# Boundary between the two layers cut from 14 steps to 11, row work through full PSUM pairs, and the last residual sum made by an accumulating DMA

## The chip, the cores and the metric

The kernel runs on one core of one Trainium2 chip. The metric is the device time of one execution in microseconds (us), lower is better. The profile of one execution shows TensorE (PE, with its weight loads as PEld), VectorE (DVE), ScalarE (ACT), GpSimd (POOL) and the DMA queue of SyncE (SP).

## The reference, cut to what matters

A batch of one sequence, 1024 rows by 1024 features in float32, passes two layers. Each layer is `x = x + rms_norm(mixer(rms_norm(x, pre_g)), post_g)`.

```python
for l in range(2):
    h = rms_norm(x, pre_norm_g[l])
    if l == 0:   # heads A (differential, 4) and B (sliding window, 8) beside each other
        y = concat([ya * silu(ga), yb * silu(gb)]) @ w_out_ab
    else:        # C: chunked attention over 9 chunks, 16 heads, relative-position bias
        y = (yc * silu(gc)) @ w_out_c
    x = x + rms_norm(y, post_norm_g[l])
```

Each of q, k, v and the gates is a projection `h @ w_in` of the normalised rows. So nothing of layer 2 can be projected for a row before layer 1 is complete for that row: its output sum, two norms and a transpose.

## The kernel before, in words

All products run on TensorE with each float32 operand cut into a high and a low part, three matmuls for one product (hi*hi, hi*lo, lo*hi). The cut of the weights is made by GpSimd (`split`, L906 the high part, four instructions on L913 the low part), the cut of everything that comes out of PSUM by ScalarE (high) and VectorE (low).

The work is laid out by hand in numbered steps. Every engine walks through the same steps in order and issues in each what the tables name for it; semaphores carry the true dependences. The units are A[0..3] (20 steps each), B[0..7] (8 steps each, steps 80 to 143), then a boundary of `BRIDGE` = 14 steps (144 to 157), then C[0..7] (20 steps each, C[0] from step 158). An attention item of a unit starts in each of its first 16 steps (8 for B): `score` (L1192), the lowest value on VectorE (L1555), the exponential on ScalarE (L1287), `turn` (the transposition of the probabilities, L1162), their cut (L1316 on ScalarE, L1619 on VectorE), `times_v` (L1118), a gate (`gated` on VectorE L1669, `hi_of_gated` on ScalarE, `gated_lo` on VectorE), and the output projection `out_matmuls` (L1045).

Between items TensorE works on fills. A fill is 24 matmuls of 128x512 (L1037, `project`) that make one half (f=0: rows 0 to 3 of 128, f=1: rows 4 to 7) of q, k, v or gate of one unit. `segment` and `segment_by` say how many of these matmuls each step gets. Fills go in turn to two PSUM banks (`dense` 0 and 1). Their weights lie in two high slots (`w_hi`) used in turn: the split of one block may start only when the last fill that used the same slot is finished. `split` stands in GpSimd's queue at a step of its own, behind the roots of the norms of that step.

The third bank (`dense` 2) serves the output projections, one half row at a time, and in the same way the transposes that bring the second layer's normalised rows back (`spare_use`). Each use waits until the one before has been read. If a step has two uses, one goes ahead of the step's fill matmuls (EARLY) and one behind (LATE).

`NORM` gives for each of the 8 rows the steps of the norm between the layers: `ysq` (square sum on ScalarE, L1431), root on GpSimd (L936, L939), `yg` (times g_post, VectorE L1748), `x1` (times the root, plus the row of x, L1758), `xsq` (square sum, L1441), root, `scaled` (L1769), `turn` (8 transposes, L1070, then high part L1360 and low part L1502). Row 4 has the steps 147, 148, 149, 149, 150, 153; rows 5 and 6 start two steps later each, row 7 starts at 153. `x1` is stored by SP to a DRAM tensor of its own (L881).

At the end rows leave in pairs (2,3), (4,5), (6,7), (0,1): `last_out` (matmuls L1045, sum into y by VectorE L1539), square sum (ScalarE L1449), root (GpSimd L936, L939), `fin = y * g_post` (VectorE L1778), `fin = fin * root + x1` (VectorE L1786) with x1 loaded back from DRAM by SP (L889), and the store by SP (L893).

## Time and profile before

| | us |
|---|---|
| median of 3 runs | 1276.82 (1276.34 to 1278.11) |
| the profiled execution, its own time | 1275.72 |
| its span | 1273.9 |
| PE busy | 1193.9 (94%) |
| DVE busy | 816.6 (64%) |
| ACT busy | 584.7 (46%) |
| POOL busy | 423.9 (33%) |
| mean granted clock of PE, of full speed | 0.982 |

The profiled execution took 1275.72 us, of which 1273.9 us is the span from the first to the last recorded event. A busy share is the mean over the whole execution. PE matmuls overlap in the records, so a 128x512 matmul shows as some 0.39 us long although the next one starts earlier; what counts is how many start in a stretch. "Idle before, releaser" names for how long the engine had nothing and what ended that.

### The profile page before, as it was taken

To read this page: it belongs to the slowest core of one execution; us is meant where nothing else is said; L and a number is where in the kernel's file an instruction comes from. 1 tells how busy PE (TensorE), PEld (TensorE's weight loads), DVE (VectorE), ACT (ScalarE), POOL (GpSimd) and SP (SyncE) were. 2 spreads that over 40 slices of the span, in tenths; PEclk is the share of its full clock that TensorE was granted. 3 is DMA by queue.
4 is the path that set the end of the run, shared out by engine and by line. 5 is a ranking of instruction groups with operands and counts; after the bars stand their busy time and mean duration, and the time that the engine had idled before them with its cause. 6 is when DMAs were issued, how large, how long until landed. Compare 5 with 4: busy or idle time off the path is not lost. (4 is left out here: it accounts for less than half of the span.)

```text
span 1273.9 us, 17678 instructions
## 1 busy us (share of the span) xinstructions
PE 1193.9 (94%) x6480; PEld 1016.0 (80%) x6480; DVE 816.6 (64%) x1726; ACT 584.7 (46%) x1296; POOL 423.9 (33%) x554
## 2 busy tenths in 40 slices
PE   6999999999999997996989999999999999999884
PEld 5978888888888886775767888888888888788773
DVE  4574755747666677766343765848658486585577
ACT  5544443444455565543354444534444444354442
POOL 5333123231364366456532213132131321313212
PEclk9999999999999998999999999999999999999987
DMA  6252111110122243152211102021020210202042
GB/s 203 68 183 60 40 34 33 34 50 17 51 67 67 67 121 111 51 154 83 83 50 55 50 17 71 17 70 34 17 71 18 70 34 18 70 19 70 17 165 99
DMA packets 95621, 83.14 MB, mean 65 GB/s; under 512 B 3216, under 2 KB 85136, under 8 KB 95536
## 3 DMA queue, kind: packets, MB, share of 16 engines
q1 hardware_dynamic: 95536, 82.02, 20.7%
q8 instruction: 52, 0.85, 0.3%
q14 instruction: 33, 0.27, 0.1%
HBM read 73.57 MB, written 13.68 MB: 68 GB/s over the span
## 5 line engine op out<-in xcount | busy, mean ns | idle before, releaser
L1037 PE MATMUL dense<-hT_hi,w_hi 128*128 128x512 f32 x880 | 351.3, 399 | 0.8 <-DVE k_l L1494 0.8
L1037 PE MATMUL dense<-hT_lo,w_hi 128*128 128x512 f32 x880 | 346.6, 394 | 0.0
L1037 PE MATMUL dense<-hT_hi,w_lo 128*128 128x512 f32 x880 | 345.3, 392 | 0.0
L906 POOL TENSOR_SCALAR w_hi<-w_f 128x1024 fp32r<-128x1024 f32 x88 | 95.6, 1086 | 671.6 <-PE dense L1037 570.8
L1287 ACT ACTIVATE e_sb<-e_sb,low 128x256 f32<-128x256 f32 (+7 forms) x256 | 170.2, 665 | 220.8 <-DVE low L1555 220.4
L913 POOL TENSOR_TENSOR w_lo<-w_f,w_hi 128x256 fp32r<-128x256 f32 x352 | 264.7, 783 | 7.3
L1316 ACT ACTIVATE pT_hi<-turned 128x640 fp32r<-128x640 f32 (+3 forms) x224 | 117.3, 524 | 189.2 <-PE pv_ps L1118 106.6
L1037 PEld LDWEIGHTS dense<-hT_hi,w_lo 128*128 128x128 f32 x880 | 166.3, 189 | 36.5
L1037 PEld LDWEIGHTS dense<-hT_hi,w_hi 128*128 128x128 f32 x880 | 166.8, 189 | 27.4 <-issue 1.0
L1037 PEld LDWEIGHTS dense<-hT_lo,w_hi 128*128 128x128 f32 x880 | 166.8, 190 | 25.0
L1619 DVE TENSOR_TENSOR pT_lo<-turned,pT_hi 128x640 fp32r<-128x640 f32 (+3 forms) x224 | 133.4, 596 | 46.4 <-ACT pT_hi L1316 45.5
L1555 DVE CUSTOM_DVE_ANT_0 e_sb<-scores,bias 128x640 f32<-128x640 f32 (+3 forms) x192 | 131.4, 685 | 46.4 <-PE scores L1192 44.3
L1162 PE MATMUL turned<-ident,e_sb 128*128 128x128 f32 x744 | 120.0, 276 | 12.2 <-DVE pT_lo L1619 11.9
L1118 PE MATMUL pv_ps<-pT_hi,v_st 128*128 128x256 f32 x536 | 129.9, 290 | 1.0 <-DVE pT_lo L1619 1.0
L1192 PE MATMUL scores<-k_hh,q_st 128*128 128x384 f32 (+3 forms) x352 | 126.8, 360 | 2.5 <-DVE q_st L1488 1.6
L1162 PEld LDWEIGHTS turned<-ident,e_sb 128*128 128x128 f32 x744 | 93.4, 141 | 43.3 <-DVE pT_lo L1619 19.2
L1118 PE MATMUL pv_ps<-pT_lo,v_st 128*128 128x256 f32 x456 | 118.2, 285 | 0.0
L1192 PE MATMUL scores<-k_l,q_st 128*128 128x384 f32 (+3 forms) x352 | 108.5, 317 | 0.0
L1118 PEld LDWEIGHTS pv_ps<-pT_hi,v_st 128*128 128x128 f32 x536 | 98.7, 193 | 2.8 <-DVE pT_lo L1619 1.4
L1532 DVE TENSOR_TENSOR y<-dense,y 128x512 f32<-128x512 f32 x116 | 79.7, 687 | 30.7 <-PE dense L1045 29.4
L1045 PE MATMUL dense<-w_hi,yT_hi 128*128 128x512 f32 x208 | 84.0, 404 | 14.9 <-DVE yT_lo L1680 8.5
L1494 DVE TENSOR_TENSOR k_l<-dense,k_hh 64x512 fp32r<-64x512 f32 x48 | 33.0, 688 | 96.2 <-ACT k_hh L1280 95.7
(154 smaller groups left out, 1757.7 us busy)
## 6 DMA issues: line engine op xcount, KB each, us to landing
w_f<-in_w_in_c SPq DMA_DIRECT2D x38, 512.0 KB, 4.0
w_f<-in_w_in_ab SPq DMA_DIRECT2D x34, 512.0 KB, 4.0
rel_tiles_dram<-rel_rows_dram SPq DMA_DIRECT2D x1, 5120.0 KB, 22.7
bias<-rel_tiles_dram SPq DMA_DIRECT2D x8, 640.0 KB, 5.3
y<-in_x SPq DMA_DIRECT2D x8, 512.0 KB, 7.7
w_f<-in_w_out_ab SPq DMA_DIRECT2D x8, 512.0 KB, 3.9
hT_lo_f<-in_x SPq DMA_DIRECT2D x8, 512.0 KB, 7.1
x_dram<-y SPq DMA_DIRECT2D x8, 512.0 KB, 2.7
```

The source lines that it names most:

```text
L906: ts(hi, src, 1.0, 1.0, ALU.mult, ALU.mult).then_inc(w_hi_done, 1)
L913: last = tt(lo[:, h, cols], src[:, h, cols], hi[:, h, cols], ALU.subtract)
L1037: last = mm(dense[:, x.n % 2, :], lhs[:, d * P:(d + 1) * P], rhs[:, d, x.f * HALF:(x.f + 1) * HALF], start=i == 0, stop=i == 23)
L1045: last = mm(bank, lhs[:, c:c + P], rhs, start=m == n == 0, stop=m == len(parts) - 1 and n == 2)
L1118: last = mm(pv_ps[:, p.n % 2, :], v_st[:, which, kt, :], p_part[:, kt - p.t + 6 - pT_set(p), :], start=i == 0 and m == 0, stop=i == p.coun ...
L1162: last = nc.tensor.transpose(turned[:, at0:at0 + P], e_sb[:, e0:e0 + P], ident[:])
L1192: last = mm(scores[:, at0:at0 + w], q_st[:, it.h, c:c + P], k_part[:, kh, key:key + w], start=i == 0, stop=i == 1)
L1287: copy(e, e, ACT.Exp, scale=-1.0, bias=stat_col(low, it.j), accum_out=stat_col(total, it.j)).then_inc(s_exp, 1)
L1316: copy(pT_hi[:, r, q], turned_tile(x), ACT.Copy).then_inc(s_thi, 1)
L1532: last = tt(into, dense[:, 2, :], into, ALU.add)
L1555: nc.vector.tensor_tensor_reduce(out=e_of(it), in0=scores[:, it.off:it.off + it.n * P], in1=bias_of(it), scale=-u.slope(it.h), scalar=star ...
L1619: tt(pT_lo[:, r, q], turned_tile(x), pT_hi[:, r, q], ALU.subtract).then_inc(s_tlo, 1)
```

## The change

1. `BRIDGE` goes from 14 to 11. The fill matmuls per step of the boundary and of C[0] are laid out anew, and one fill more is in that segment: q of C[1], first half, moved out of the four dense steps behind C[0]. It shares its weights with q of C[1], second half, which stays there, now last.
2. The outputs of B[6] and B[7] for rows 4 to 7 and the turning of these rows leave the third bank. `row_use` gives each row a whole PSUM pair of 1024 columns (`turned` and `scores` in turn, free at that time): 12 matmuls in one go, one sum of 1024 columns, later 8 transposes, one copy, one subtraction.
3. `NORM` starts earlier and closer for all 8 rows; rows 0 to 3 turn their two halves in different steps. The last gate of B[7] and its `times_v` come one step earlier.
4. The first layer's result is stored in `out` itself. At the end `fin = (y * root) * g_post` is one VectorE instruction, and GpSimd issues a DMA that adds `fin` to what is stored in `out`. The instruction L1778, the eight loads back and SP's stores of `fin` go.
5. In C[7] the gates come a step earlier, rows 4 and 5 leave at steps 12 and 13 (were 14, 15), rows 6 and 7 at 16 and 17 (were 18, 19) with squares and sums put behind the last gate (19 and 20), rows 0 and 1 at 20 and 21 (were 22, 23).

```diff
-BRIDGE = 14
+BRIDGE = 11
-TOTAL = C[7].start + 27
+TOTAL = C[7].start + 24
...
-                pv_ = Pv(u_, h_, t_ - 1, len(PVS), g_.step + (2 if u_.kind == "B" else 1), g_)
+                pv_ = Pv(u_, h_, t_ - 1, len(PVS), g_.step + (2 if u_.kind == "B" and not (u_ is B[7] and t_ == 7) else 1), g_)
...
-                        g_ = pv_.step + (1 if u_ is B[7] else 2)
-                        GATES.append(Gate(u_, len(GATES), g_, slice(c_, c_ + 2 * P), pv_, len(RECS) - 1,
-                                          g_ + (0 if u_ is B[7] else 1)))
+                        soon_ = u_ is B[7] or u_ is C[7]
+                        g_ = pv_.step + (1 if soon_ and it_.step > u_.step(3) or u_ is B[7] else 2)
+                        GATES.append(Gate(u_, len(GATES), g_, slice(c_, c_ + 2 * P), pv_, len(RECS) - 1, g_ + (0 if soon_ else 1)))
...
 segment_by([("k", C[0], 0), ("v", C[0], 0), ("g", C[0], 0), ("v", C[1], 0), ("k", C[0], 1), ("q", C[0], 1),
-            ("v", C[0], 1), ("g", C[0], 1), ("v", C[1], 1)], c_ - BRIDGE,
-           5 * [4] + 4 * [5] + 5 * [9] + [14, 15, 15, 15] + 4 * [12] + 8 * [3])
+            ("v", C[0], 1), ("g", C[0], 1), ("v", C[1], 1), ("q", C[1], 0)], c_ - BRIDGE,
+           [6, 5] + 4 * [4] + 5 * [12] + [9] + 9 * [10] + 6 * [9])
...
-        segment(both("k", C[i_ + 1]) + both("q", C[i_ + 1]), C[i_].step(16), C[i_].step(19))
+        segment(both("k", C[i_ + 1]) + (both("q", C[i_ + 1]) if i_ else [("q", C[1], 1)]), C[i_].step(16), C[i_].step(19))
...
-out_steps((B[6], B[7]), [(s_ - BRIDGE + 1 + t, 1) for t in range(8)])
...
-NORM = [Row(0, *b_steps(4.6, 4.7, 5.1, 5.2, 5.4, 5.6)), Row(1, *b_steps(5.1, 5.2, 5.4, 5.5, 5.7, 6.1)),
-        Row(2, *b_steps(5.5, 5.6, 6.0, 6.1, 6.3, 6.5)), Row(3, *b_steps(6.0, 6.1, 6.5, 6.6, 7.0, 7.2))]
+NORM = [Row(0, *b_steps(4.5, 4.6, 4.7, 5.1, 5.3, 5.5)), Row(1, *b_steps(5.0, 5.1, 5.2, 5.3, 5.6, 5.7)),
+        Row(2, *b_steps(5.2, 5.4, 5.5, 5.6, 6.0, 6.1)), Row(3, *b_steps(5.5, 5.7, 6.1, 6.2, 6.4, 6.5))]
...
-    ((3, 4, 5, 5, 6, 9), (5, 6, 7, 7, 8, 10), (7, 8, 9, 9, 10, 11), (9, 10, 11, 11, 12, 13)), 4)]
+    ((3, 4, 4, 5, 6, 7), (4, 5, 5, 6, 7, 8), (5, 6, 6, 7, 8, 9), (6, 7, 7, 8, 9, 10)), 4)]
+for n_, late_ in zip(NORM[:4], b_steps(5.6, 6.0, 6.2, 7.2)):
+    SPARE_RAW += [(n_.turn, "turn", (), n_.r, 0), (late_, "turn", (), n_.r, 1)]
...
+ROW_USES = [RowUse(n_, "out", 4 + n_, s_ + 2 + n_) for n_ in range(4)]
+ROW_USES += [RowUse(4 + n_, "turn", 4 + n_, NORM[4 + n_].turn) for n_ in range(4)]
...
+for k_, (p_, outs_, squared_, summed_) in enumerate(((1, (10, 11), (11, 12), (12, 13)), (2, (12, 13), (13, 14), (14, 15)),
+                                                     (3, (16, 17), (19, 19), (20, 20)), (0, (20, 21), (21, 22), (22, 23)))):
...
     @block.gpsimd
+            for x in FINAL:
+                if s == x.summed:
+                    if new(f_sum, x.n + 1):
+                        pool.wait_ge(f_sum, x.n + 1)
+                    if new(n_stored, 16 * ST):
+                        pool.wait_ge(n_stored, 16 * ST)
+                    nc.gpsimd.dma_start(out[rows_of(x.row), :], fin[:, x.row, :], accum_op=ALU.add).then_inc(f_stored, 16)
...
     @block.tensor
+        def row_use(x):
+            if x.n < 2:
+                if new(s_low, B_LAST.j + 1):
+                    pe.wait_ge(s_low, B_LAST.j + 1)
+                if new(s_tlo, G_OF_ITEM[B_LAST].idx + 1):
+                    pe.wait_ge(s_tlo, G_OF_ITEM[B_LAST].idx + 1)
+            if new(r_free, x.n - 1):
+                pe.wait_ge(r_free, x.n - 1)
+            if x.what == "out":
...
+                for half in range(2):
+                    last = out_matmuls(row_bank(x)[:, half * HALF:(half + 1) * HALF],
+                                       [(yT_hi, yT_lo, w.u.col(x.row), hi_place(w.hi)[:, half, :], lo_place(w.slot)[:, half, :])
+                                        for w in ROW_BLOCKS])
+            else:
+                if new(n_scaled, x.row + 1):
+                    pe.wait_ge(n_scaled, x.row + 1)
+                for d in range(DT):
+                    last = nc.tensor.transpose(row_bank(x)[:, d * P:(d + 1) * P], x_place(x.row)[:, d, :], ident[:])
+            last.then_inc(r_filled, 1)
...
     @block.vector
+            if x.what == "out":
+                if new(r_filled, x.n + 1):
+                    dve.wait_ge(r_filled, x.n + 1)
+                tt(y[:, x.row, :], row_bank(x)[:], y[:, x.row, :], ALU.add).then_inc(r_free, 1)
...
-                tt(fin[:, row, :], y[:, row, :], g_post[:], ALU.mult).then_inc(f_yg, 1)
...
-                stt(out=fin[:, row, :], in0=fin[:, row, :], scalar=rowstat[:, 2, row:row + 1], in1=x1_back[:, row, :],
-                    op0=ALU.mult, op1=ALU.add).then_inc(f_sum, 1)
+                    stt(out=fin[:, x.row, :], in0=y[:, x.row, :], scalar=rowstat[:, 2, x.row:x.row + 1], in1=g_post[:],
+                        op0=ALU.mult, op1=ALU.mult).then_inc(f_sum, 1)
```

## Rows read from the trace of the kernel before

**Rows 1.** The page, its first line.

```profile
span 1273.9 us, 17678 instructions
```

**Rows 2.** The chain that ended last, its end: start, length, what.

```profile
1260.35 2.92 PE dense L1045 x6
...
1269.61 1.28 DVE fin L1786
```

**Rows 3.** Busy time by stretch: length, PE busy (instructions), clock, DMA share, GB/s.

```profile
488.50:528.00 39.50, 29.84 (x155) 0.87 0.22 76
560.70:619.60 58.90, 43.64 (x199) 0.94 0.28 91
619.60:676.40 56.80, 48.09 (x275) 1.00 0.20 59
1215.00:1273.90 58.90, 37.29 (x171) 0.79 0.31 124
```

**Rows 4.** The same view for the instructions of L1037 alone, one fill.

```profile
676.40:681.90 5.50, 5.50 (x24) 4.32 (x24) 1.00 0.24 71
```

**Rows 5.** Timeline of PE in B[5] and B[6]: second halves of rows 0, 1.

```profile
496.74 1.12 PE L1070 MATMUL dense<-ident,hT_lo_f 128*128 128x128 f32 x4 [4.16 <-DVE hT_lo L1502]
...
509.28 1.11 PE L1070 MATMUL dense<-ident,hT_lo_f 128*128 128x128 f32 x4 [2.50 <-DVE hT_lo L1502]
```

**Rows 6.** Timeline of PE in the boundary; the last is C[0]'s first score.

```profile
564.96 0.47 PE L1045 MATMUL dense<-w_hi,yT_hi 128*128 128x512 f32 x1 [2.97 <-DVE yT_lo L1680]
...
587.08 0.54 PE L1045 MATMUL dense<-w_hi,yT_hi 128*128 128x512 f32 x1 [4.03 <-DVE y L1532]
...
619.55 0.22 PE L1192 MATMUL scores<-k_hh,q_st 128*128 128x128 f32 x1
```

**Rows 7.** Groups by line and form, 560 to 620 us: busy, mean ns | idle before.

```profile
L1748 DVE TENSOR_TENSOR y<-y,g_post 128x1024 f32<-128x1024 f32 x4 | 5.0, 1246 | 0.0
...
L939 POOL TENSOR_TENSOR rowstat<-rowstat,mhalf 128x1 f32<-128x1 f32 x8 | 4.4, 549 | 0.7
...
L1431 ACT ACTIVATE junk<-y 128x1024 bf16<-128x1024 f32 x4 | 4.2, 1056 | 9.4 <-DVE y L1532 9.4
...
L1280 ACT ACTIVATE k_hh<-dense 64x512 fp32r<-64x512 f32 x4 | 2.4, 592 | 0.1
```

**Rows 8.** Timeline of POOL: one split of weights in the boundary.

```profile
581.00 1.05 POOL L906 TENSOR_SCALAR w_hi<-w_f 128x1024 fp32r<-128x1024 f32 x1
582.14 5.43 POOL L913 TENSOR_TENSOR w_lo<-w_f,w_hi 128x256 fp32r<-128x256 f32 x4
```

**Rows 9.** The same four instructions by line: ns min/median/max.

```profile
L913 POOL TENSOR_TENSOR w_lo<-w_f,w_hi x4: 722/734/3362, 582.1 to 586.8; 128x256 fp32r<-128x256 f32 x4
```

**Rows 10.** Timeline of DVE beside that split.

```profile
583.89 1.21 DVE L1748 TENSOR_TENSOR y<-y,g_post 128x1024 f32<-128x1024 f32 x1
585.02 1.28 DVE L1769 SCALAR_TENSOR_TENSOR hT_lo_f<-y,rowstat,g_pre 128x1024 f32<-128x1024 f32 x1
```

**Rows 11.** Waits of PE, 620 to 703 us: total, times, longest.

```profile
PE turned L1162 <- DVE pT_lo L1619: 6.5, 6, 1.5
PE turned L1150 <- DVE pT_lo L1619: 1.4, 1, 1.4
```

**Rows 12.** Timeline of PE at the last `turn_rec`.

```profile
1246.48 0.69 PE L1129 MATMUL pv_ps<-ident,rec_wide 128*128 128x128 f32 x2 [3.52 <-ACT rec_wide L1353]
```

**Rows 13.** Timeline of DVE at the last gate.

```profile
1250.39 0.42 DVE L1603 TENSOR_TENSOR o_sb<-o_sb,pv_ps 128x256 f32<-128x256 f32 x1
...
1255.80 0.42 DVE L1669 SCALAR_TENSOR_TENSOR o_sb<-o_sb,gate 128x256 f32<-128x256 f32 x1
```

**Rows 14.** DMA issues: count, KB, median us to landing.

```profile
w_f<-in_w_in_c SPq DMA_DIRECT2D x38, 512.0 KB, 4.0
...
x_back<-x_dram SPq DMA_DIRECT2D x8, 512.0 KB, 7.3
```

**Rows 15.** The stores of the output, by tile.

```profile
DMA to landing us min/median/max: 2.6/2.6/3.0
```

More of the change, by code:

```diff
@@ L469 @@
     own_ = (3, 4) if u_ in B[1:7:2] else (4, 5) if u_ is B[7] else (2, 3)
+    if u_ in B[6:]:
+        w_ = Block("o", u_, 0, 0, ROW_USES[0].step, *own_)
+        w_.done = ("row", 4, ROW_USES[3].step)
+        O_BLOCKS.append(w_)
+        continue
     w_ = Block("o", u_, 0, 0, OUTS[u_][0].step, *own_)
@@ L536 @@
 FILLS_AT = {s: [f for f in FILLS if f.drain == s] for s in range(TOTAL)}
+ROW_AT = {s: at(ROW_USES, s) for s in range(-1, TOTAL)}
 LAST_AT = {s: [x for x in LAST_OUTS if x[0] == s] for s in range(TOTAL)}
@@ L541 @@
 DENOMINATORS_AT = {s: [(r, it) for r, it, _ in RECS if it.step + 2 == s] for s in range(TOTAL)}
-def final_rows(s, lag):
-    return [(n, row) for a, n, row in FINAL if a + lag == s]
 def gate_of(u, row):
@@ L694, in program @@
         sem(f"norm_{k}") for k in ("ysq", "ymean", "yr", "yscaled", "sum", "xsq", "xmean", "xr", "scaled", "hi"))
+    r_filled, r_hi, r_free = sem("row_filled"), sem("row_hi"), sem("row_free")
     f_filled, f_free = sem("last_filled"), sem("last_free")
[L696 removed]
+    f_sq, f_mean, f_r, f_sum = (sem(f"final_{k}") for k in ("sq", "mean", "r", "sum"))
     f_stored = sem("out_stored")
@@ L806, in freed_by @@
                 what, value, _ = done
-                if new({"fill": s_filled, "spare": s_spare, "pro": p_filled}[what], value - (PRO_USES if what == "spare" else 0)):
-                    sp.wait_ge({"fill": s_filled, "spare": s_spare, "pro": p_filled}[what], value - (PRO_USES if what == "spare" else 0))
+                if new({"fill": s_filled, "spare": s_spare, "pro": p_filled, "row": r_filled}[what], value - (PRO_USES if what == "spare" else 0)):
+                    sp.wait_ge({"fill": s_filled, "spare": s_spare, "pro": p_filled, "row": r_filled}[what], value - (PRO_USES if what == "spare" else 0))
         def load_x(i):
@@ L880, in _ @@
                         sp.wait_ge(n_sum, n.r + 1)
[L881 to L893 removed]
+                    sp.dma_start(out[rows_of(n.r), :], y[:, n.r, :]).then_inc(n_stored, 16)
         if new(f_stored, 16 * ST):
@@ L928, in freed_by @@
             what, value, _ = done
-            if new({"fill": s_filled, "spare": s_spare, "pro": p_filled}[what], value - (PRO_USES if what == "spare" else 0)):
-                pool.wait_ge({"fill": s_filled, "spare": s_spare, "pro": p_filled}[what], value - (PRO_USES if what == "spare" else 0))
+            if new({"fill": s_filled, "spare": s_spare, "pro": p_filled, "row": r_filled}[what], value - (PRO_USES if what == "spare" else 0)):
+                pool.wait_ge({"fill": s_filled, "spare": s_spare, "pro": p_filled, "row": r_filled}[what], value - (PRO_USES if what == "spare" else 0))
         def inverse_root(src_done, n, src, mean, done_mean, into, done, scale):
@@ L1215, in _ @@
                 spare_use(x)
+            for x in ROW_AT[s]:
+                row_use(x)
             for x in TURNED_AT[s]:
@@ L1335, in hi_of_gated @@
                 act.wait_ge(s_y, g.n + 1)
-            older = [x.use for u in UNITS[:g.u.n] for x in OUTS[u] if same_columns(slice(u.col(x.row), u.col(x.row) + P), g.cols)]
+            older = [x.use for u in UNITS[:g.u.n] for x in OUTS.get(u, []) if same_columns(slice(u.col(x.row), u.col(x.row) + P), g.cols)]
             if g.u is C[7]:
@@ L1389, in _ @@
                     hi_of_rows(x)
+            for x in ROW_AT[s - 1]:
+                if x.what == "turn":
+                    hi_of_row(x)
             for x in TURNED_AT[s - 1]:
@@ L1533, in spare_use, with row_use @@
             last.then_inc(bank_free[2], 1)
+        def row_use(x):
+            if x.what == "out":
+                if new(r_filled, x.n + 1):
+                    dve.wait_ge(r_filled, x.n + 1)
+                tt(y[:, x.row, :], row_bank(x)[:], y[:, x.row, :], ALU.add).then_inc(r_free, 1)
+            else:
+                if new(r_hi, x.n - 3):
+                    dve.wait_ge(r_hi, x.n - 3)
+                part = (slice(None), slice(None), rows_of(x.row))
+                tt(hT_lo[part], row_bank(x)[:].rearrange("p (d s) -> p d s", d=DT), hT_hi[part], ALU.subtract).then_inc(r_free, 1)
         def last_out(n, row, half):
@@ L1713, in _ @@
                 spare_use(x)
+            for x in ROW_AT[s - 1]:
+                row_use(x)
             for it in ITEMS_AT.get(s - 1, []):
```

129 lines of the change are left out of this document (73 added, 56 removed).

## The prediction

> **What bounds the kernel now.** I read the page first: the span is 1273.9 us [rows 1], and TensorE is busy for 1193.9 us of it (the table). The reader should see that a change can only win where TensorE waits, or works at the lower clock, some 80 us in all. The chain of waits [rows 2] shows only the last few us, so I went on to busy time by stretch [rows 3], which tells where the waits lie. Between 488.5 and 528 us TensorE is idle for 39.5 - 29.8 = 9.7 us, in the boundary (560.7 to 619.6) for 58.9 - 43.6 = 15.3, in C[0] (619.6 to 676.4) for 56.8 - 48.1 = 8.7, and in the last 58.9 us for 21.6. In the first, second and fourth the mean granted clock is 0.87, 0.94 and 0.79: part of the work there runs at the lower level (1.2 GHz, where full is 2.4). Behind C[0] TensorE is full: 24 fill matmuls take 5.50 us [rows 4], 0.229 us each. The timelines then name each wait's end. All this the change touches, and nothing else: the matmuls are the same in number.
>
> **Rows 0 to 3, in B[4] to B[6].** Before, both halves of a row turn in one step, so the second half must wait until ScalarE and VectorE have emptied the bank: 4.16 and 2.50 us for rows 0 and 1 [rows 5]. After, the halves stand in different steps, and no step has two of VectorE's long norm instructions (before, x1 of row 1 and scaled of row 0 shared a step). Ceiling: the 9.7 us, and about (1 - 0.87) x 30 = 3.9 us of slow clock. Floor: nothing, if VectorE, which then has the same work in less time, makes the waits again. I take the two named waits less a little that comes back, 6 us. Range 0 to 11.
>
> **The boundary, step 144 to C[0]'s first score.** I give times on the clock of before, so that gains add. VectorE's gate of step 144 is unchanged, and its low part lets TensorE start row 4 at 564.96 [rows 6] before. After, the row stands in step 146 and waits for the last turned item; the 7 fill matmuls more ahead of it cover most of that. I get a start at 566.9. Then 12 matmuls for each row (2.75 us) and 4 fill matmuls (0.9) alternate; two whole PSUM pairs mean that no row waits for the sum of the row before, so the 4.03 us wait [rows 6] goes. Row 7 is done at 581.8, against 592.8 before, with 13 fill matmuls (3 us) fewer: 8 us ahead.
>
> Next is what I count as the catch: GpSimd's queue. The split of the gate weights of C[0] stands in step 150 in both kernels. Before, they are needed in step 153, now in step 151, 9 matmuls in, which TensorE reaches at 581.8 + 21 x 0.229 = 586.6. In GpSimd's queue the split stands behind the roots of row 7's first and row 5's second norm. Their squares stand on ScalarE behind k of C[0] (4 x 0.59, from 581.8 to 584.2) and take 1.15 each (1.06 and the read of the sum) [rows 7], to 586.5; two instructions of a root are 0.19 + 0.55 and gaps, to 587.3. The split itself takes 1.05 + 4 x 0.72 and gaps = 3.9 us undisturbed, so the weights are there at 591.2 at best: a wait of 4.6 us on TensorE. But a split before took 1.05 + 5.43 [rows 8], because one of its four instructions, 0.73 us by the median, took 3.36 [rows 9] while VectorE ran two norm instructions with both inputs in SBUF [rows 10]. After, VectorE has six of these one behind the other from 585.5 to 592.8 (1.15 to 1.25 us each [rows 7, 10]). If GpSimd gets in only when they pause for a root, the weights come at about 598. I take 594.5, between the two, and 1.9 us for a clock that falls behind such a wait (before, 0.94 over the stretch cost (1 - 0.94) x 43.6 = 2.6 us [rows 3]).
>
> The Trainium skill, SBUF — State Buffer, section Who interferes with whom, says that a VectorE instruction with two SBUF inputs blocks a GpSimd instruction that reads SBUF fully, whoever is second. The trace agrees in the one instruction of 3.36 us. By that rule alone the weights would come at the late end, which is rival (b).
>
> From 594.5: 3 matmuls and row 4's turn to 597.8; then three steps of 12 matmuls (2.75) and a turn (1.1), and 9 matmuls, gives the first score at 611.5 to 612. Before it is 619.55 [rows 6], with 3 fill matmuls more done. Gain 8 - 0.7 and 0.6 for the second wait at v's transposes = 6.4 us. Range 3 (weights at 598) to 10.5 (at 591.2, no clock lost).
>
> **C[0] and the seam to C[1].** In C[0] TensorE waits 6.5 us in six waits for the low part of the probabilities and 1.4 for v's transposes [rows 11], all in steps that have 3 fill matmuls. Now these have 9 or 10: 6 more are 1.4 us, longer than the waits of 1.0 to 1.5. So 27 more matmuls (6.2 us) go into C[0], and its length stays at about 56.5 us; the 1.4 stays too. The four steps behind it lose 24 matmuls, 5.5 us, of which 0.2 + 5.5 is the gain. But the order there is now k, k, q: q's second half is last, and it holds the high slot that the gate weights of C[1] need. Their split can start only when q is finished (before, it ran beside q's 11 us), and the first gate fill is the next thing TensorE has. That is a new wait of 3.9 us less the 1.1 of v's transposes in front = 2.8, with a part of a us for the clock. Net gain 5.7 - 2.8 = 2.9, I take 3.0. Range 1 to 5.5.
>
> Nothing else in the middle changes: SP's eight loads back and GpSimd's mask are moved to where their engines have idle time, and the store of x1 goes to another tensor by the same DMA.
>
> **The end.** Before, VectorE is free for the last gate at 1250.8, but gates at 1255.80 [rows 13], since row 6's sums and the product stand in front; and the output of rows 0 and 1 starts at 1260.35 [rows 2]. After, rows 6 and 7 are multiplied in steps 16 and 17, where TensorE waited 3.52 and 1.03 us [rows 12]. Laying the new order out with the durations above I get: `times_rec` at 1251.4, gate 1251.8, its low part ready at 1252.9, row 0 on TensorE from then. VectorE must take the final products of rows 6 and 7 first (squares and roots behind each other, to 1257.9), then the sums of rows 0 (to 1259.1) and 1 (1260.9), the product of row 0, the root of row 1, and its product to 1264.4. Before, this last instruction ends at 1269.61 + 1.28 = 1270.9 [rows 2], 6.5 later. Per row an instruction of 1.23 us less is in this.
>
> Behind it stands the last DMA. Before 3.0 us to the end of the span [rows 15]. An accumulating DMA from GpSimd is not in the trace. Bounds: as the store, 3.0; as a queued load back of the same rows and a store behind it, 7.3 + 3.0 = 10.3 [rows 14, 15]. A lone load is 4.0 [rows 14], which gives 7.0 with the store. I take 6.0, since reading and writing overlap by rows and GpSimd has to make the descriptors. Gain 6.5 - 3.0 = 3.5, range 0 to 6.5 (it cannot be under -0.8 by the bound).
>
> The Trainium skill, DMA: Bandwidth & Descriptors, section Anatomy of one DMA, fits 2.0 us + bytes / 436 GB/s for a DMA of this path, an estimate of 3.2 us for 512 KB; by that the sum would be 2.8 us better. No row here shows it.
>
> **Sum.** 6 + 6.4 + 3.0 + 3.5 = 18.9 us. The profiled execution took 1275.72, so 1256.8; the median of the runs is 1.1 higher than it, so 1257.9, said as 1258.
>
> **The rivals.**
> (a) *More than that*: splits get through between VectorE's instructions, and the waits in B[5] and B[6] go with their clock losses. 10 + 10 + 3.5 + 5 = 28.5: 1248. For it: GpSimd's small instructions got in beside VectorE's in other places. Against: six in a row. Chance 0.17.
> (b) *The weights take the gain of the boundary* (weights at 598 and again late for v of C[1], +2 us at the seam): boundary 2, seam 1, B stretch 4, end 2.5: 9.5, 1267. For it: the 3.36 us instruction. Against: the chain itself pauses for roots of GpSimd. Chance 0.2.
> (c) *Slower*: the accumulating DMAs are slow. Each must read and write 512 KB, and four are issued in the last 10 us. The place is the end; it decides if the last landing is more than 3 + 15.4 + 6.5 = 25 us behind VectorE's last instruction. At 8 us per DMA in series from 1256, the four would end at 1288 on the old clock, 15.4 less is 1273: still not slower. It takes 11 us each for 1285. The longest landing of 512 KB in the rows is 7.3, of queued ones [rows 14]. Chance 0.05.
> (d) *The change doesn't do what it says*: the row steps are closer on paper, but the norm chain of ScalarE, GpSimd, VectorE is as long as before and the first score comes when it did, 619; the stretch of rows 0 to 3 too. Then only seam and end count, 6.5: 1270. Against: before, the rows waited for the half-row bank, not for the chain. Chance 0.06.
>
> **The numbers.** The likeliest case has 0.52 and 1254 to 1263 as its own range. From (a) to (b) with the bounds of the last DMA gives 1248 to 1268, outside which lie (c), (d) and tails of (a) and (b), 2 in 10. This measurement can tell 0.2%, 2.6 us, from no change. Faster by more: 0.92; within: 0.04; slower: 0.04, each from the tails of (c) and (d).
>
> **What the profile after would show.** Right: second halves of rows 0 and 1 without waits; row sums of 1024 columns 1.28 us long; TensorE waiting 5 to 10 us in the boundary on w_lo of GpSimd, in front of a fill, with one split over 5 us there; the first score 13 us or so earlier (6 + 6.4); no waits over 0.5 us for pT_lo in C[0]'s last six steps; a wait of about 3 us on GpSimd at the first gate fill of C[1]; VectorE's last instruction 22 us earlier than 1270.9; 4 to 8 us behind it. Wrong: a boundary without a wait for w_lo, or one for the scaled rows instead; GpSimd held for several us by each DMA issue, so that roots come late; a span that ends over 10 us behind the last product.

## The result, and the profile after

The changed kernel takes 1269.1 us (median of four runs, 1268.99 to 1271.52), the kernel before 1276.86 beside it: a ratio of 0.9942, 95% interval 0.9925 to 0.996. The gain is 7.8 us where 18.9 were forecast, and the time lies 1.1 us outside the range. Run once more beside other kernels it gave 1269.77, ratio 0.9953 (0.9938 to 0.9968). Two executions in all, 1382.43 us of the kernel before and 1363.26 us of one experiment, ran at a granted clock of 0.83 and 0.84 and count in no ratio.

The profiled execution of the changed kernel took 1271.52 us and is the slowest of its four, that of the kernel before took 1275.72. So the two profiles below are 4.2 us apart, where the medians are 7.8 apart.

The page, first line, and the end of the chain that ended last:

```profile
span 1269.7 us, 17644 instructions
```

```profile
1256.42 1.29 DVE fin L1867
1257.72 0.29 issue
1258.01 0.89 POOL out_x L999
1258.90 4.92 issue
1263.82 0.90 POOLq L616
```

Against [rows 2] VectorE's last product ends 13.2 us earlier, at 1257.7, but the span goes on for 12.0 us behind it and not for 3.0. Of these, 4.92 stand between two DMA issues of GpSimd, in which the profile shows nothing that GpSimd waits for.

Busy time by stretch (columns as in [rows 3]); the stretches are those of [rows 3], moved to where the work now lies:

```profile
488.50:528.00 39.50, 30.50 (x171) 0.96 0.24 80
558.60:615.60 57.00, 42.27 (x191) 0.88 0.29 94
615.60:670.90 55.30, 53.64 (x305) 1.00 0.24 67
1210.80:1269.70 58.90, 31.12 (x145) 0.77 0.46 71
```

C[0] is what was forecast: idle for 1.7 us instead of 8.7 [rows 3]. The boundary is not: idle for 14.7 us, as before, with a lower clock. The timeline of PE names the waits, first in the B stretch, then in the boundary to C[0]'s first score:

```profile
490.92 0.66 PE L1095 MATMUL dense<-ident,hT_lo_f 128*128 128x128 f32 x4 [1.43 <-DVE y L1607]
494.95 0.66 PE L1095 MATMUL dense<-ident,hT_lo_f 128*128 128x128 f32 x4 [0.82 <-DVE hT_lo L1577]
499.16 0.66 PE L1095 MATMUL dense<-ident,hT_lo_f 128*128 128x128 f32 x4 [1.73 <-DVE hT_lo L1577]
...
506.94 0.66 PE L1095 MATMUL dense<-ident,hT_lo_f 128*128 128x128 f32 x4 [2.08 <-DVE hT_lo L1577]
```

```profile
564.91 0.47 PE L1070 MATMUL scores<-w_hi,yT_hi 128*128 128x512 f32 x1 [1.79 <-DVE pT_lo L1705]
...
595.76 0.79 PE L1062 MATMUL dense<-hT_hi,w_hi 128*128 128x512 f32 x1 [9.70 <-POOL w_lo L926]
...
608.25 0.50 PE L1062 MATMUL dense<-hT_hi,w_hi 128*128 128x512 f32 x1 [2.74 <-POOL w_lo L926]
...
615.63 0.22 PE L1249 MATMUL scores<-k_hh,q_st 128*128 128x128 f32 x1
```

The waits of [rows 5] and the 4.03 of [rows 6] are gone. In place of the first stand smaller ones, one for a row sum (1.43) and three for the same low parts, in place of the second one of 9.70 us for the gate weights and one of 2.74 for v of C[1]. What holds them is in GpSimd's timeline, with VectorE's beside it:

```profile
585.10 1.35 POOL L949 TENSOR_SCALAR rowstat<-rowstat 128x1 f32<-128x1 f32 x1 [2.27 <-ACT junk L1505]
586.53 0.55 POOL L952 TENSOR_TENSOR rowstat<-rowstat,mhalf 128x1 f32<-128x1 f32 x1
587.16 0.68 POOL L949 TENSOR_SCALAR rowstat<-rowstat 128x1 f32<-128x1 f32 x1
587.93 1.47 POOL L952 TENSOR_TENSOR rowstat<-rowstat,mhalf 128x1 f32<-128x1 f32 x1
589.38 1.65 POOL L919 TENSOR_SCALAR w_hi<-w_f 128x1024 fp32r<-128x1024 f32 x1
591.11 4.59 POOL L926 TENSOR_TENSOR w_lo<-w_f,w_hi 128x256 fp32r<-128x256 f32 x4
...
601.79 0.89 POOL L949 TENSOR_SCALAR rowstat<-rowstat 128x1 f32<-128x1 f32 x1 [5.17 <-ACT junk L1515]
...
604.41 3.79 POOL L926 TENSOR_TENSOR w_lo<-w_f,w_hi 128x256 fp32r<-128x256 f32 x4
```

```profile
590.22 1.88 DVE L1846 SCALAR_TENSOR_TENSOR y<-y,rowstat,hT_lo_f 128x1024 f32<-128x1024 f32 x1
```

The split of the gate weights begins at 589.38, behind two roots, and ends at 595.7. The second split stands behind the root of row 7's second norm, which waits 5.17 us for a square on ScalarE. That square, at 600.55, is itself behind the copy of row 4's turn, and the turn behind TensorE's first wait. So the first wait hands on a second one.

Waits of PE, 620 to 703 us, for [rows 11]: the six waits for `pT_lo` are gone, and the seam's is there, 3.2 where 2.8 was forecast (the 1.5 for v's transposes stays).

```profile
PE dense L1062 <- POOL w_lo L926: 3.2, 1, 3.2
```

The fourth and the eighth DMA issue on GpSimd (timeline), and their landing (the view by source), for [rows 15]:

```profile
1235.17 0.88 POOL L999 DMA_DIRECT2D out_x<-fin  x1 [5.06 <-issue]
...
1263.85 0.87 POOL L999 DMA_DIRECT2D out_x<-fin  x1 [4.95 <-issue]
```

```profile
DMA to landing us min/median/max: 5.2/5.6/6.6
```

The points that the timelines give, in us; "again" is the second profile of the changed kernel, "part 3 undone" and "part 4 undone" are experiments below:

| | before | after | again | part 3 undone | part 4 undone |
|---|---|---|---|---|---|
| last score of B[7] | 558.69 | 556.53 | 555.33 | 558.66 | 555.46 |
| first score of C[0] | 619.55 | 615.63 | 614.80 | 618.15 | 616.47 |
| first score of C[1] | 704.72 | 698.34 | 697.73 | 700.42 | 699.00 |
| second v turn of C[7] | 1201.37 | 1193.03 | 1192.21 | 1195.86 | 1194.05 |
| end of VectorE's last product | 1270.89 | 1257.70 | 1257.48 | 1260.56 | 1264.50 |
| end of the span | 1273.9 | 1269.7 | 1268.1 | 1272.6 | 1267.5 |

Differences of its rows are the lengths of the stretches. The boundary, from the first row to the second, takes 60.9 us before and 59.1, 59.5, 59.5 and 61.0 with the new one. Two experiments below that leave its code alone (q first, and the room for descriptors) have 60.6 and 60.8. What sets these six apart is the granted clock behind two waits of TensorE: the one for the last turned item, at 564.91 above, and the second one for weights, at 608.25. Busy time of 4 us behind the first and of 6 us behind the second, in the changed kernel, in its repeat, and with q first:

```profile
564.90:568.90 4.00, 3.99 (x12) 0.69 0.00 1
608.20:614.20 6.00, 5.95 (x34) 1.00 0.12 35
```

```profile
563.70:567.70 4.00, 4.00 (x22) 1.00 0.00 0
605.80:611.80 6.00, 5.98 (x23) 0.72 0.21 64
```

```profile
564.20:568.20 4.00, 3.96 (x11) 0.57 0.00 0
607.60:613.60 6.00, 6.00 (x23) 0.72 0.02 5
```

With one fall of the clock the boundary takes 59.1 to 59.5 us (part 3 undone is the third), with both 60.6 to 61.0 (q first, the room, part 4 undone). The first wait is 1.79 us in the changed kernel, where the clock falls, and 1.79 in its repeat, where it doesn't. So a stretch of a single profile can differ by 1.5 us for each such fall, whatever the edit.

### The profile page after: what moved, and what is told of

It is laid out like the page before. It is cut to its first block, busy times and chain, and to the rows that moved or that the text cites. A ratio compares the mean times of both kernels' runs of the same rounds, so it can differ in the third digit from the quotient of the medians.

```text
span 1269.7 us, 17644 instructions
## 1 busy us (share of the span) xinstructions
PE 1187.9 (94%) x6480; PEld 1012.3 (80%) x6480; DVE 805.3 (63%) x1710; ACT 584.5 (46%) x1292; POOL 428.1 (34%) x562
## 4 chain that ended last, share of the span: by engine, by line
PE 44%; DVE 4%; ACT 3%; POOL 2%; issue 2%; POOLq 0%; DVEq 0%; ACTq 0%
PE dense L1062 23%; PE dense L1070 6%; PE pv_ps L1169 5%; PE scores L1249 4%; PE turned L1216 4%; POOL w_lo L926 1%; DVE o_sb L1755 1%; DVE yT_lo L1766 1%; PE turned L1204 1%; ACT junk L1524 1%; DVE pT_lo L1705 1%; ACT yT_hi L1407 0%; ACT v_st L1362 0%; DVE e_sb L1641 0%; ACT pT_hi L1375 0%
## 5 line engine op out<-in xcount | busy, mean ns | idle before, releaser
L1070 PE MATMUL dense<-w_hi,yT_hi 128*128 128x512 f32 x200 | 80.3, 402 | 10.2 <-DVE yT_lo L1766 5.6
L1607 DVE TENSOR_TENSOR y<-dense,y 128x512 f32<-128x512 f32 x108 | 74.2, 687 | 23.1 <-PE dense L1070 21.6
```

Source lines behind the costliest of these rows:

```text
L1070: last = mm(bank, lhs[:, c:c + P], rhs, start=m == n == 0, stop=m == len(parts) - 1 and n == 2)
L1607: last = tt(into, dense[:, 2, :], into, ALU.add)
```

## The experiments

**Split one step earlier.** The splits of steps 149 to 153 lose the step that the code adds to them; the gate weights' stands in step 149 in place of 150.

```
-        if B[5].start <= w_.split <= C[0].start + 8:
+        if B[5].start <= w_.split <= C[0].start + 8 and not (chain_ is ROTATION and 149 <= w_.split <= 153):
             w_.split += 1
```

> The changed kernel, with three weight splits one step earlier in GpSimd's queue (gate of C[0] in step 149 instead of 150, v of C[1] 151 instead of 152, k of C[0] 153 instead of 154), so that they stand ahead of the roots that wait for ScalarE. Theory (the queue order causes the two waits of 9.70 and 2.74 us in the boundary): the gate split starts at about 583 instead of 589.4, TensorE's wait there falls to 3 us or less, the second wait goes, and 8 to 11 us are won. Rival (VectorE's norm instructions hold GpSimd off, wherever the split stands): the split takes over 8 us in place of 6.2, the first wait stays over 6 us, and no more than 5 us are won. Second rival (the norm chain binds behind it): the waits for weights go, but waits for the scaled rows of as much take their place; under 3 us won.

Measured: 1263.83 us, 0.9902 (0.9889 to 0.9916), 5.3 to 5.9 less than the changed kernel, between the theory (8 to 11) and the rival (under 5). Timeline of PE, and of POOL for both splits and a later one, in this kernel:

```profile
589.79 0.79 PE L1062 MATMUL dense<-hT_hi,w_hi 128*128 128x512 f32 x1 [4.31 <-POOL w_lo L926]
```

```profile
583.37 6.37 POOL L926 TENSOR_TENSOR w_lo<-w_f,w_hi 128x256 fp32r<-128x256 f32 x4
...
596.61 3.67 POOL L926 TENSOR_TENSOR w_lo<-w_f,w_hi 128x256 fp32r<-128x256 f32 x4
...
616.13 2.82 POOL L926 TENSOR_TENSOR w_lo<-w_f,w_hi 128x256 fp32r<-128x256 f32 x4
```

VectorE beside the second of them:

```profile
595.99 1.61 DVE L1857 SCALAR_TENSOR_TENSOR hT_lo_f<-y,rowstat,g_pre 128x1024 f32<-128x1024 f32 x1
```

The first wait falls from 9.70 to 4.31, the second is gone, and C[0]'s first score comes at 607.69, 51.8 us behind B[7]'s last score in place of 59.1. The same four instructions take 6.37 us beside four of VectorE's norm instructions, 3.67 beside one of them, and 2.82 with none beside them. So both are shown: the place in the queue made most of the wait, and VectorE's norms still hold the split up where it now stands.

**q of C[1] ahead of k at the seam.**

```
-    segment(both("k", C[i_ + 1]) + (both("q", C[i_ + 1]) if i_ else [("q", C[1], 1)]), C[i_].step(16), C[i_].step(19))
+    segment(both("k", C[i_ + 1]) + both("q", C[i_ + 1]) if i_ else [("q", C[1], 1)] + both("k", C[1]), C[i_].step(16), C[i_].step(19))
```

> The changed kernel, with q's second half of C[1] put ahead of k in the four steps behind C[0], so that its weight slot is free while k is filled. Theory (the gate weights of C[1] come late because their slot is held until the last fill): the wait of 3.18 us at C[1]'s first gate fill goes, with the slower clock behind it: 3.2 to 4 us won. Rival (the wait is VectorE's and ScalarE's emptying of the banks in that place, and would come back at the next fill): under 1 us.

Measured: 1268.10 us, 0.9936 (0.9922 to 0.9949), 1.0 to 1.7 less than the changed kernel, with intervals that overlap. The wait of 3.18 is gone; a new one opens 6 us on, for the low part of a gate (timeline of PE):

```profile
701.68 0.48 PE L1070 MATMUL dense<-w_hi,yT_hi 128*128 128x512 f32 x1 [1.69 <-DVE yT_lo L1766]
```

From C[0]'s last score to C[1]'s first it is 23.0 us instead of 27.5, but from there to C[7]'s v turn 496.4 instead of the 494.5 to 495.4 of the kernels with k first: 1.0 to 1.9 of the 4.5 are given back. The boundary of this profile is at its long end (60.6), which hides another 1.5.

**Three times the room for DMA descriptors.** Bytes per partition, with the first address behind them.

```
-dynamic_dma_scratch_size=1024
+dynamic_dma_scratch_size=3072
-    top = [1152]
+    top = [3200]
```

> The changed kernel, with 3072 bytes of each SBUF partition reserved for the descriptors of GpSimd's DMAs instead of 1024. Theory (the fourth and the eighth accumulating DMA wait until the one before has landed because the space for descriptors is used up): both issue as soon as their row is ready, the waits of 5.06 and 4.95 us before them go, the span ends about 6.5 to 7 us behind VectorE's last instruction instead of 12.0, and 5 us are won. Rival (two accumulating DMAs into the same output cannot be in flight together, or GpSimd waits for its own landing for another reason): the waits stay, nothing won.

Measured: 1267.50 us, 0.9931 (0.9917 to 0.9945), 1.6 to 2.3 less than the changed kernel, again with overlapping intervals. The same two issues on GpSimd:

```profile
1234.94 0.85 POOL L999 DMA_DIRECT2D out_x<-fin  x1 [3.23 <-DVE fin L1867]
...
1259.66 0.85 POOL L999 DMA_DIRECT2D out_x<-fin  x1 [0.79 <-DVE fin L1867]
```

Both waits for "issue" are gone; GpSimd now waits for VectorE's product. From the last product to the end it is 7.35 us, not 12.0 (10.6 in the repeat). In this profile the boundary was at its long end too (60.8, against 59.1), which hides some 1.5 of it in the span; that it did so in the other executions isn't shown. So 3.3 to 4.7 of the 12.0 were the room, and 7.3 are the accumulating DMA itself.

**All three edits together.**

> The three edits together. If each of the three theories holds, the gains add: 16 to 20 us under the changed kernel, some 1250 us. If one wait stands behind another (the emptying of banks, the norm chain), the sum is less than that of the three alone.

Measured: 1256.27 us, 0.9846 (0.9831 to 0.9861). 12.8 less than the changed kernel; alone they gave 5.3, 1.0 and 1.6, which is 4.9 less than that. The profiles add up better: the spans are 7.5, 2.3 and 3.0 shorter alone and 13.2 together. The second wait of the boundary is 2.25 to 3.43 us where the splits have their old step, and 0.54 here. With it goes the fall of the clock behind it, which the two small edits each had in their profiles; that may give up to 3 of the 4.9, and the rest is open. The last product ends at 1249.17, the span at 1256.5.

**The changed kernel again.**

> The changed kernel once more, as the measure for the three that run beside it. All theories: its median of 1269.1, within 0.2% (1266.6 to 1271.6). One thing more is read from its profile: the middle of the kernel, from C[1]'s first score to C[7]'s second v turn, gave 2.0 us in the first profile of the changed kernel (496.65 before, 494.69 after) with no edit there. If that is a real effect of the changed order it is 494.7 again; if it is scatter between profiled executions it lands anywhere between 494 and 497.

Measured: 1269.77. The middle took 494.48 us (494.69 in the first profile, 496.65 before). It is 494.9 to 495.4 in four more kernels with the new order and k first, so the 2.0 come again. No edit stands there, but the clock differs. The busy time of 12 us behind the same wait, by windows, before (wait of 1.99 us) and after (1.92), and in the kernel with all three edits (2.15):

```profile
1106.00:1118.00 12.00, 11.51 (x49) 0.86 0.00 0
```

```profile
1099.00:1111.00 12.00, 11.29 (x57) 1.00 0.00 0
```

```profile
1089.00:1101.00 12.00, 11.38 (x49) 0.86 0.00 0
```

The clock falls behind it in the first and third, not in the second: 49 matmuls in 12 us and not 57. From this wait to the next one it is 11.4 us with the fall (11.44, 11.46) and 9.9 without, which is 1.5 of the 2.0 to 2.2. Among the kernels with q first the clock falls here in some (the three edits, part 5 undone, the last row in halves) and not in others (q first alone, part 4 undone on the three edits, both kernels with the splits ahead of the roots), and the middle is 498.0 to 498.3 in the first and 496.3 to 496.4 in the second. None of the edits between these stands at this wait, so the 1.5 are not a gain that the change was made for.

**Part 3 undone.** Rows 0 to 3 and both their half turns back on their old steps; rows 4 to 7 and the last gate of B[7] keep the new ones.

```
-NORM = [Row(0, *b_steps(4.5, 4.6, 4.7, 5.1, 5.3, 5.5)), Row(1, *b_steps(5.0, 5.1, 5.2, 5.3, 5.6, 5.7)),
-        Row(2, *b_steps(5.2, 5.4, 5.5, 5.6, 6.0, 6.1)), Row(3, *b_steps(5.5, 5.7, 6.1, 6.2, 6.4, 6.5))]
+NORM = [Row(0, *b_steps(4.6, 4.7, 5.1, 5.2, 5.4, 5.6)), Row(1, *b_steps(5.1, 5.2, 5.4, 5.5, 5.7, 6.1)),
+        Row(2, *b_steps(5.5, 5.6, 6.0, 6.1, 6.3, 6.5)), Row(3, *b_steps(6.0, 6.1, 6.5, 6.6, 7.0, 7.2))]
...
-for n_, late_ in zip(NORM[:4], b_steps(5.6, 6.0, 6.2, 7.2)):
+for n_, late_ in zip(NORM[:4], b_steps(5.6, 6.1, 6.5, 7.2)):
```

> Part 3 alone is undone: the norms of rows 0 to 3 and the two half turns of each row go back to their old steps, the rest is as in the changed kernel. Theory 1 (part 3 is worth what the profile of the changed kernel shows, 2.2 us in the B stretch, and all of it reaches the end): 1271.3, and the last score of B comes 2.2 later than beside it. Theory 2 (the forecast's 6 us are there, and the other 3.8 were eaten by another part, for example by the missing out-product work of B[6] and B[7] that now runs behind the scores): 1275. Theory 3 (what is gained in B is lost again in the boundary, because GpSimd's splits, not TensorE, set the first score of C[0]): last score of B 2.2 later, but C[0]'s first score unchanged and the time 1269.

Measured: 1273.72 us, 0.9979 (0.997 to 0.9988), 4.0 more than the changed kernel beside it (3.3 by the ratios): between theory 1 and theory 2. The two waits of [rows 5] are back (timeline of PE):

```profile
496.50 1.11 PE L1095 MATMUL dense<-ident,hT_lo_f 128*128 128x128 f32 x4 [4.16 <-DVE hT_lo L1577]
...
509.06 0.66 PE L1095 MATMUL dense<-ident,hT_lo_f 128*128 128x128 f32 x4 [2.79 <-DVE hT_lo L1577]
```

B[7]'s last score comes at 558.66, as before the change (558.69). So part 3 is worth 3.3 us against the profile of the changed kernel beside it, 2.1 against the first one, and 3.3 to 4.0 in the time. Nothing else moved the B stretch. The boundary has the same 59.5 us as in the profile beside it, so the gain is handed through whole and theory 3 is out.

**Part 4 undone.** x1 to a scratch tensor and back by SyncE's loads, the product with `g_post` ahead of the root, the sum in VectorE's last instruction, stores by SyncE; the new steps stay.

```
+                    tt(fin[:, x.row, :], y[:, x.row, :], g_post[:], ALU.mult).then_inc(f_yg, 1)
...
-                    stt(out=fin[:, x.row, :], in0=y[:, x.row, :], scalar=rowstat[:, 2, x.row:x.row + 1], in1=g_post[:],
-                        op0=ALU.mult, op1=ALU.mult).then_inc(f_sum, 1)
+                    stt(out=fin[:, x.row, :], in0=fin[:, x.row, :], scalar=rowstat[:, 2, x.row:x.row + 1], in1=x1_back[:, x.row, :],
+                        op0=ALU.mult, op1=ALU.add).then_inc(f_sum, 1)
...
-                    nc.gpsimd.dma_start(out[rows_of(x.row), :], fin[:, x.row, :], accum_op=ALU.add).then_inc(f_stored, 16)
```

> Part 4 alone is undone: x1 goes to a scratch tensor and is loaded back, VectorE makes y times g_post ahead of the root and adds in the last instruction, SyncE stores; the new order and steps of the end stay. Theory 1 (the accumulating DMA costs 12.0 us behind the last product where a plain store costs 3.0, and the plain way costs nothing elsewhere): 9.0 less than the changed kernel, 1260, with 3.0 from the last product to the end of the span. Theory 2 (the eight products more on VectorE and the eight loads push the last product back by some of 8 x 1.2 us; say by 4): 1264. Theory 3 (the store is as slow by either way, since the time is memory's and not the queue's): 1269.

Measured: 1269.08 us, 0.994 (0.9928 to 0.9952), the same as the changed kernel. Theory 3 named this time, but not for its reason. The store is 9.0 us quicker behind the last product (3.0), and the product comes later: 70.4 us behind C[7]'s second v turn, not 64.7 to 65.3. Timeline of DVE at its end:

```profile
1260.08 1.22 DVE L1875 TENSOR_TENSOR fin<-y,g_post 128x1024 f32<-128x1024 f32 x1
1261.23 1.28 DVE L1884 SCALAR_TENSOR_TENSOR fin<-fin,rowstat,x_back 128x1024 f32<-128x1024 f32 x1
1263.22 1.28 DVE L1884 SCALAR_TENSOR_TENSOR fin<-fin,rowstat,x_back 128x1024 f32<-128x1024 f32 x1 [0.72 <-POOL rowstat L967]
```

VectorE has eight more products of 1.22. In the time part 4 is neutral: what it takes from VectorE, the slower landing takes back. In the profiles it costs: from C[7]'s second v turn to the end of the span it is 73.5 us here, 76.7 and 75.9 in the changed kernel, and 72.5 before. The boundary of this profile, 61.0, is 1.5 longer than in the repeat and hides part of that.

**The three edits with part 4 undone.**

> The three edits of the best kernel so far (split one step earlier, q of C[1] ahead of k, 3072 bytes for descriptors), and part 4 undone on top. The best kernel so far took 1256.3, with 7.3 us from its last product to its end. Theory 1 (a plain store ends 3.0 behind the last product): 4.3 less, 1252.0. Theory 2 (the eight products more on VectorE cost what the store gives back): 1256. Theory 3 (the gains do not add, a wait for the loads back of x1 opens): above 1257.

Measured: 1257.25 us, 0.9847 (0.9834 to 0.986), level with the three edits alone. Once the room is enough, part 4 takes 5.8 us from the way to the last product and adds 4.3 behind it (the three edits against this kernel). These 1.5 us in its favour are in the profiles, and the ratios, 0.9846 and 0.9847, don't show them.

**Part 5 undone, on the three edits.** Steps of C[7]'s gates, outs, squares and sums as before.

```
-for k_, (p_, outs_, squared_, summed_) in enumerate(((1, (10, 11), (11, 12), (12, 13)), (2, (12, 13), (13, 14), (14, 15)),
-                                                     (3, (16, 17), (19, 19), (20, 20)), (0, (20, 21), (21, 22), (22, 23)))):
+for k_, (p_, outs_, squared_, summed_) in enumerate(((1, (10, 11), (11, 12), (12, 13)), (2, (14, 15), (15, 16), (16, 17)),
+                                                     (3, (18, 19), (19, 20), (20, 21)), (0, (22, 23), (23, 24), (24, 25)))):
```

Cut out here: the gates' steps, which go back likewise.

> On the kernel with the three edits (split one step earlier, q ahead of k, 3072 bytes; 1256.3 us, 64.7 from C[7]'s second v turn to VectorE's last product), part 5 alone is undone: the outs, squares and sums of C[7]'s pairs and C[7]'s gates go back to their steps of before; the accumulating DMA stays. Theory 1 (the forecast: part 5 and part 4 together bring VectorE's last instruction 6.5 forward; leaving out y times g_post and the loads gives part of it, the new steps the rest): the way from the v turn to the last product goes back to 67 to 69.5, the time to 1259 to 1261. Theory 2 (the kernel with part 4 undone showed 70.4 on this way against 69.5 before, so the new steps bring nothing and all of the gain is the product left out): 64.7 and 1256. Theory 3 (the new steps cost, since rows 3 and 0 are now finished later behind the last gate): below 1255.

Measured: 1256.62 us, 0.9835 (0.9822 to 0.9848), the same as with the three edits: theory 2. From the v turn to the last product 65.0 us with the old steps, 64.7 with the new.

**Splits ahead of the roots of their step.**

```
+            if 149 <= s <= 151:
+                splits_of(s)
             for n in NORM:
...
-            for w in SPLITS_AT.get(s, []):
-                freed_by(w.hi_free)
-                split(PRO_SPLITS + w.n, w.hi, w.slot, w.loads)
+            if not 149 <= s <= 151:
+                splits_of(s)
```

`splits_of` holds the three lines taken out. All else is as in the kernel with the three edits.

> On the same kernel GpSimd makes the splits of steps 149 to 151 ahead of the roots of the same step, so that the gate weights of C[0] no longer stand behind the root of row 4's second norm. TensorE's wait there was 4.3 us; the k fills before it ended at 581.2, the split began at 582.65 and took 7.5 for what takes 4.7 elsewhere. Theory 1 (the wait is what the split's order leaves over plus its slowing beside VectorE): the split begins 1.3 to 1.4 earlier, the wait falls to about 3 and the time by 1.3, to 1255. Theory 2 (the roots put off hold VectorE's norms of rows 4 to 7, and the turns of these rows, not the weights, now set C[0]'s first score): the wait falls, but a wait for hT_lo_f or at the turns opens, and the time stays within 0.1%.

Measured: 1254.46 us, 0.9819 (0.9806 to 0.9832). POOL and PE:

```profile
575.96 1.04 POOL L919 TENSOR_SCALAR w_hi<-w_f 128x1024 fp32r<-128x1024 f32 x1
577.08 4.67 POOL L926 TENSOR_TENSOR w_lo<-w_f,w_hi 128x256 fp32r<-128x256 f32 x4
```

```profile
587.77 1.09 PE L1127 MATMUL scores<-ident,hT_lo_f 128*128 128x128 f32 x4 [3.81 <-DVE hT_lo_f L1863]
```

The split begins 6.7 us earlier than with the three edits (582.65), and 4.7 earlier in the next kernel but one, which has the same edit, where 1.3 to 1.4 were expected: it had stood behind roots that were waiting for squares. (The 4.7 of a split "elsewhere" is one beside a norm instruction; with none it is 1.05 and 2.82.) The weights' wait is gone, and the row chain's (theory 2) is in its place, 3.81 us for the scaled row 4.

So little is won in the boundary. It takes 49.4 us here and 51.5 in that later kernel, against 50.0 to 51.8 in five profiles with the three edits' splits or the first edit alone. The shorter value of each range has no fall of the clock behind the boundary's first wait, the longer one has. Like with like the edit gives 0.6 to 0.9 without the fall and 0.1 to 0.3 with it. The time is 1.8 less than with the three edits, and 2.2 and 3.0 less than the two kernels run beside it. Of these, the fall in the middle (1.5 to 1.6), which this profile doesn't have, is no gain of the edit.

**The last row tile in two halves.** On the kernel with the three edits; on VectorE and, likewise, GpSimd:

```
+                    for part in (slice(0, D),) if x.n < 7 else (slice(0, HALF), slice(HALF, D)):
+                        stt(out=fin[:, x.row, part], in0=y[:, x.row, part], scalar=rowstat[:, 2, x.row:x.row + 1], in1=g_post[:, part],
+                            op0=ALU.mult, op1=ALU.mult).then_inc(f_sum, 1)
```

> On the same kernel the last row tile's product and accumulating DMA are cut into two halves of 128 x 512 (256 KB each). Behind the last product the span had 7.3 us: 0.9 of issue, 5.2 to 6.6 of landing, and the rest. Theory 1 (landing of an accumulating DMA is mostly moving bytes, twice over): the second half lands in about 3.5, and the time falls by 1.5 to 2. Theory 2 (mostly fixed latency, read and then write): nothing falls, 1256.3 within 0.1%, or it rises by the second issue's 0.9.

Measured: 1257.48 us, 0.9838 (0.9824 to 0.9851), nothing. From the last product to the end it is still 7.5 us. The two halves, in flight together, land 6.0 and 6.6 us from their issues, where the other seven DMAs of 512 KB take 5.3 to 6.2: half the bytes land no sooner.

**The last two row tiles by load and store, on the fastest kernel.**

```
-            for x in FINAL:
+            for x in FINAL[:6]:
                 if s == x.summed:
...
                     nc.gpsimd.dma_start(out[rows_of(x.row), :], fin[:, x.row, :], accum_op=ALU.add).then_inc(f_stored, 16)
```

The other two take the lines of "Part 4 undone"; their x1 is read back from the output tensor.

> On the fastest kernel so far (the one with GpSimd's splits ahead of the roots, 1254.5 us or 0.9819 of before; 7.6 us from VectorE's last product to the end of the span) only the last two row tiles go the way of before: their x1 is loaded back early, VectorE makes y times g_post while ScalarE squares, its last instruction adds, and SyncE stores; the first six keep the accumulating DMA. Theory 1 (the plain store ends 3.0 behind its product, the two products more lie beside the squares and the roots, and the six accumulating DMAs land before): 3.5 to 4.5 less, 1250.0 to 1251.0, with 3.0 behind the last product. Theory 2 (as in the kernel with part 4 undone, where the whole way was 5.8 longer for eight such products: the last two alone cost most of it): 1254 or more. Theory 3 (the loads and stores of SyncE meet the accumulating DMAs in the queues): the store takes over 4 us and the time is 1252 to 1254.

Measured: 1251.3 us, 0.9793 (0.9779 to 0.9806), the fastest of all, 25 to 26 us less than before. The span is 1250.3 us. Timeline of DVE at its end:

```profile
1242.76 1.23 DVE L1885 TENSOR_TENSOR fin<-y,g_post 128x1024 f32<-128x1024 f32 x1
1243.90 1.28 DVE L1894 SCALAR_TENSOR_TENSOR fin<-fin,rowstat,x_back 128x1024 f32<-128x1024 f32 x1
1245.90 1.28 DVE L1894 SCALAR_TENSOR_TENSOR fin<-fin,rowstat,x_back 128x1024 f32<-128x1024 f32 x1 [0.72 <-POOL rowstat L973]
```

The last product still waits 0.72 for its root, so the product of 1.23 more lies beside the square and the root; the end comes 3.1 behind it, where it came 7.6 behind it in the kernel with all eight added.

## Why the prediction was wrong

It failed at two steps, in the boundary and at the last DMA, and a third term was too large. (A small slip of its sum: 8 less 0.7 less 0.6 is 6.7 and not 6.4. And its "some 80 us" counts only idle time, not the slower clock.)

- **B stretch, 6 us: mis-sized.** Part 3 is worth 3.3 to 4.0 us in the time, 2.2 and 3.4 are measured in the profiles. The two waits of 4.16 and 2.50 do go, but the "little that comes back" is most of them: single half turns wait 1.43, 0.82, 1.73 and 2.08 us. PE is idle for 9.0 us in the stretch against 9.7; the clock, 0.96 in place of 0.87, brings most of the gain (an estimate: 0.09 of 30 us, 2.7).
- **Boundary, 6.4 us: the failed step is "I take 594.5".** On the clock of before (2.2 us later here) the weights were ready at 597.9, the late end of the forecast, and the forecast's own sum from there gives 615.5, its bound of 3. It wasn't the split itself that was priced too low. It took 6.3 us, where 594.5 had left it 7.2. It began at 591.5 and not at 587.3. The squares ahead of the roots came 1.8 us late: row 7 was done 1.5 late, with the clock at 0.69 behind a wait of 1.79. And the two roots, priced at 0.74 each, took 2.0 and 2.2 beside VectorE's norms. The rest is the second wait of 2.74, which the likeliest case did not have. Measured, the boundary gives -0.2 to 1.8 in six profiles of the same code. The price of the queue's order is shown: one step earlier gives 5.3 to 5.9 in the time.
- **C[0] and the seam, 3.0 us: right.** 2.5 and 2.2 measured; C[0] keeps its length with 27 matmuls more, and the new wait is 3.18 where 2.8 was said. Taken away, 1.0 to 1.9 of it come back, with a wait of 1.69 at the next gate.
- **Middle, 0: off by 2.0,** 1.5 of it a clock that fell behind one wait before and not after. That is luck: in later kernels it falls or not with no edit there.
- **End, 3.5 us: the failed step is "I take 6.0" for the last DMA.** It is 12.0 and 10.6. 7.3 are the DMA's own, 0.9 of issue in it; the rest is a wait of GpSimd for room for descriptors, which no bound of the forecast had (it named the sign, a span that ends over 10 us behind the last product). VectorE's last product comes 4.9 and 4.3 earlier relative to C[7], where 6.5 was said. All but 0.4 of that is the work left out by part 4. The new steps bring nothing, and with part 4 undone the way is 0.9 longer than before. The end as a whole lost 4.1 and 3.4 where 3.5 was to be won.

Sum of after, in order B, boundary, C[0] and seam, middle, last product, last DMA: 2.2 + 1.8 + 2.5 + 2.0 + 4.9 - 9.0 = 4.2 us of span (its terms are rounded), 5.8 in the repeat (medians: 7.8 and 6.4). Rival (b) described the boundary and gave 1267, but its end, 2.5 us won, was as wrong as the likeliest one's. The 1270 of (d) is near by number alone: its reason was a norm chain that bounds the first score, and what bounded it were the weights; the chain was next behind them.

Left open: why the clock falls behind a wait in one execution and not in another of the same code, and what part 2 alone brings.

## What to carry to other kernels

When work is pulled forward past a shared queue, list what stands ahead of each entry and what that in turn waits for: a ready split stood here behind a root that waited for a square, and moving it up by one step gave 5.3 to 5.9 us. Price the small entries ahead of it too, as slow as they run beside the other engine. When a wait goes, ask whose turn is next: weights first, then the chain of norms. A slower transfer that saves compute belongs where something hides it; only the last few, which nothing hides, should go the way that lands soonest. And before a difference of 1 or 2 us between two profiles is put down to an edit, compare the granted clock behind the same waits.

## What the runs showed of the hardware

- A DMA of 512 KB that adds to what is stored landed in 5.2 to 6.6 us from its issue on GpSimd in the changed kernel, plus 0.85 to 1.07 of issue there, where the plain store takes 2.6 to 3.0. 256 KB ended no sooner (7.5 against 7.3 us behind the product). The Trainium skill, DMA: Bandwidth & Descriptors, section Anatomy of one DMA, would make it an estimate of 3.2 us for 512 KB; the trace does not agree for this kind of DMA.
- With 1024 bytes per partition for descriptors, the fourth and the eighth such DMA waited 4.6 to 5.2 us on GpSimd, in five profiles; with 3072 none did.
- GpSimd's four low-part instructions took 2.82 us with no norm instruction of VectorE beside them, 3.67 beside one and 6.37 beside four. Those have two inputs in SBUF, and themselves went from 1.21 to 1.30 up to 1.74 to 1.88. A root's pair went from 0.74 to over 2 us.
- Behind nearly equal waits (1.92, 1.99, 2.15 us) the granted clock of the next 12 us was 1.00, 0.86 and 0.86, 1.5 us apart. Behind a wait of 1.79 us in two executions of the same kernel it was 0.69 and 1.00 in the next 4 us.
